# Moving half of chunk 1's index products into the first MLP group, and four weight subtractions to VectorE

## What is computed

```python
dots = jnp.einsum('bqhd,bsd->bqhs', iqb, ik) * IDX_DIM ** -0.5
score = jnp.einsum('bqh,bqhs->bqs', iwb, jax.nn.relu(dots))
score = jnp.where(causal[None], score, -jnp.inf)
_, idx = lax.top_k(score, k_sel)                      # k_sel = 256
...
mix = jnp.concatenate([pool_out, attn_out], axis=-1) @ w_o[l]
x = layer_norm(ALPHA * x + mix, ln1_g[l], ln1_b[l])
ff = jnp.square(jax.nn.relu(x @ w_up[l])) @ w_down[l]
x = layer_norm(ALPHA * x + ff, ln2_g[l], ln2_b[l])
```

## Time and profile before

| | us |
|---|---|
| median of 3 runs | 1300.05 (1298.27 to 1300.18) |
| profiled execution | 1294.91 |
| its span | 1292.9 |
| TensorE busy | 1217.0 (94%) |
| VectorE busy | 849.8 (66%) |
| ScalarE busy | 557.8 (43%) |
| GpSimd busy | 502.6 (39%) |
| mean granted TensorE clock | 0.982 |

### The profile page before, as it was taken

One profiled execution on the slowest core, in us unless ns is written; L12 is line 12 of the kernel. 1 busy time (PEld: TensorE's weight loads), 2 busy tenths in 40 slices (PEclk: granted clock), 3 DMA queues, 4 the chain that ended last, 5 costly groups with the idle time before them and its releaser, 6 DMA issues.

```text
span 1292.9 us, 17124 instructions
## 1 busy us (share of the span) xinstructions
PE 1217.0 (94%) x5639; PEld 975.7 (75%) x5639; DVE 849.8 (66%) x1322; ACT 557.8 (43%) x943; POOL 502.6 (39%) x366
## 2 busy tenths in 40 slices
PE   4999899799989999999999999989799999999997
PEld 2786686577668878778778778878688888888886
DVE  7677999766988888888989068953632232232337
ACT  3445652575525325334244266652243342442440
POOL 5534674333326666666666653204101101102002
PEclk9999899899989999999999999999899999999999
DMA  6732232030302222232332300224033323323331
GB/s 198 238 82 57 58 98 98 23 141 34 98 1 82 98 83 96 90 99 89 96 97 85 126 2 17 95 86 121 12 97 98 97 87 92 97 97 89 91 128 67
DMA packets 125724, 114.32 MB, mean 88 GB/s; under 512 B 5661, under 2 KB 99434, under 8 KB 125674
## 3 DMA queue, kind: packets, MB, share of 16 engines
q1 hardware_dynamic: 125674, 113.67, 28.2%
HBM read 105.25 MB, written 8.40 MB: 88 GB/s over the span
## 4 chain that ended last, share of the span: by engine, by line
PE 70%; DVE 16%; issue 7%; POOL 3%; ACT 2%; DVEq 1%; DMA 1%; POOLq 0%; SPq 0%; ACTq 0%
PE g_bank L1447 12%; PE g_bank L1448 12%; PE g_bank L1449 12%; PE wide L1447 10%; PE wide L1449 10%; PE wide L1448 10%; DVE score L866 3%; PE g_bank L1412 3%; DVE logit L927 1%; DVE win L548 1%; POOL rstd L703 1%; DVE probs_lo L943 1%; PE wide L1550 1%; DVE work L893 1%; POOL wo_lo L413 1%
## 5 line engine op out<-in xcount | busy, mean ns | idle before, releaser
L413 POOL TENSOR_TENSOR wlo<-wring,whi 128x1024 fp32r<-128x1024 f32 (+1 forms) x94 | 228.7, 2434 | 254.2 <-ACT whi L1331 128.6
L1447 PE MATMUL g_bank<-xhi,whi 128*128 128x512 f32 (+1 forms) x736 | 297.8, 405 | 5.5 <-DVE xlo L578 2.7
L1448 PE MATMUL g_bank<-xlo,whi 128*128 128x512 f32 (+1 forms) x736 | 293.7, 399 | 0.0
L1449 PE MATMUL g_bank<-xhi,wlo 128*128 128x512 f32 (+1 forms) x736 | 293.2, 398 | 0.0
L1331 ACT ACTIVATE whi<-wring 128x1024 fp32r<-128x1024 f32 x120 | 127.1, 1059 | 376.8 <-PE g_bank L1449 195.7
L413 DVE TENSOR_TENSOR wlo<-wring,whi 128x1024 fp32r<-128x1024 f32 (+1 forms) x66 | 88.3, 1339 | 224.6 <-ACT whi L1331 217.6
L1447 PE MATMUL wide<-whi,hhi 128*128 128x512 f32 x480 | 190.0, 396 | 1.0 <-POOL wlo L413 1.0
L1449 PE MATMUL wide<-whi,hlo 128*128 128x512 f32 x480 | 189.6, 395 | 0.0
L1448 PE MATMUL wide<-wlo,hhi 128*128 128x512 f32 x480 | 189.6, 395 | 0.0
L1447 PEld LDWEIGHTS g_bank<-xhi,whi 128*128 128x128 f32 (+1 forms) x736 | 138.9, 189 | 45.5 <-issue 5.4
L748 POOL TENSOR_TENSOR rows<-rows,y_stage 128x512 f32<-128x512 f32 x56 | 73.8, 1341 | 249.3 <-ACT y_stage L1321 248.0
(11 more groups left out here) (199 smaller groups left out, 1982.2 us busy)
## 6 DMA issues: line engine op xcount, KB each, us to landing
wring<-in_w_up SPq DMA_DIRECT2D x64, 512.0 KB, 4.2
wring<-in_w_down SPq DMA_DIRECT2D x64, 512.0 KB, 3.5
wring<-in_w_in SPq DMA_DIRECT2D x26, 512.0 KB, 3.8
wring<-in_w_o SPq DMA_DIRECT2D x16, 512.0 KB, 3.6
rows<-in_x SPq DMA_DIRECT2D x8, 512.0 KB, 4.7
normalized_rows<-rows SPq DMA_DIRECT2D x8, 512.0 KB, 4.3
rows<-normalized_rows SPq DMA_DIRECT2D x8, 512.0 KB, 6.2
out<-rows SPq DMA_DIRECT2D x7, 512.0 KB, 2.6
```

The costliest lines, as they stand in the source:

```text
L413: eng.tensor_tensor(parts_of(name, lo_tile(name)), parts_of(name, wring[n % 4]), parts_of(name, hi_tile(name)).bitcast(F32), ALU.subtract) ...
L1447: nc.tensor.matmul(out_ap, w_hi, m_hi, start=first, stop=False)
L1448: nc.tensor.matmul(out_ap, w_hi, m_lo, start=False, stop=False)
L1449: return nc.tensor.matmul(out_ap, w_lo, m_hi, start=False, stop=last)
```

## The change

1. Of the 32 index products of blocks 4 to 7, 16 stay in the output projection of chunk 0: one behind each step of half A, head by head (heads 0 to 3, each for blocks 4 to 7). The other 16 (heads 4 to 7) go into the first four up units of that chunk's MLP: three between accumulation pairs of the unit, one behind it. For this the first group is written out on TensorE, ScalarE and GpSimd (`past` and `dotted`), and its loops run one group less.
2. VectorE makes the last 16 additions after the whole residual stage and before the selections. An addition waits for that of the same block four before. GpSimd's diagonals move from before the MLP to its unit 4, behind all 48 additions; ScalarE waits for those at unit 4 too.
3. `relu_sb` moves to 40 to 48, where hidden parts 4 to 7 are written, and its neighbours to 32 to 40.
4. The parked weights of the output projection get places by chunk: in chunk 1 they lie at 32 to 64, and their high parts no longer wait for the low parts of the mix.
5. In chunk 1 the low parts of these four are made by VectorE, behind step (0, 2, 3), not by GpSimd.

```diff
-        relu_sb = part("relu_sb", 32, [P, 2, S])
-        near_up = part("near_up", 40, [P, HEADS, NEAR])
+        relu_sb = part("relu_sb", 40, [P, 2, S])
+        near_up = part("near_up", 32, [P, HEADS, NEAR])
...
-        park_at = (40, 44, 64, 68, 72, 76, 88.25, 92.25)
+        park_at = ((32, 36, 64, 68, 72, 76, 88.25, 92.25), (32, 36, 40, 44, 48, 52, 56, 60))
...
-                  or n[:2] == ("mlp", 1)]
+                  or n[:2] == ("mlp", 1) or n[:3] == ("wo", 1, 1)]
...
+        def dot_of(n):
+
+            return (n // HEADS + 2, n % HEADS) if n < 16 else ((n - 16) % CB + CB, (n - 16) // CB)
+
         def dots_after(c, nh, u, b):
 
-
-            counts = [1, 2] * 8 + [1] * 8 + [0] * 8
-            n = projection_steps().index((nh, u, b))
-            first = 16 + sum(counts[:n])
-            return [] if c else list(range(first, first + counts[n]))
+            return [16 + 4 * u + b] if c == 0 and nh == 0 else []
...
-                    pool.wait_ge(score_added, 8 * (i - 2) + 8)
+                    pool.wait_ge(score_added, 8 * (i - 2) + 8 if i < CB else 48)
...
-            diagonals((4, 5, 6, 7))
...
-            with pool.Fori(0, GROUPS - 1) as g:
+            def first_group(j):
+                if j == 4:
+                    diagonals((4, 5, 6, 7))
+                add_at(0, 0)(j)
+
+            mlp_lo(pool, 0, 0, False, first_group)
+            with pool.Fori(1, GROUPS - 1) as g:
                 mlp_lo(pool, 0, g, False, add_at(0, g))
...
-            lo(*units[U[("wo", 1, 0, 2)]:U[("mlp", 1, 0)]])
+            lo(("wo", 1, 0, 2), ("wo", 1, 0, 3))
...
-                    dve.wait_ge(score_added, n)
+                    dve.wait_ge(score_added, n if n < 16 else n - CB + 1)
...
+                    if c and (nh, u, b) == (0, 2, CB - 1):
+                        for piece in range(4):
+                            split_lo(dve, ("wo", 1, 1, piece), lo_dve)
...
             add_residual(0, LN1_0)
+            for d in range(32, 48):
+                add_score(d)
             for i in range(CB, NB):
                 select(i)
...
-                    act.wait_ge(mix_lo_ready, 8 * name[1] + 8)
+                    if name[1] == 0:
+                        act.wait_ge(mix_lo_ready, 8)
                     act.wait_ge(logits_full, 32 * name[1] + 32)
...
                     nh, u = divmod(j - GT, 4)
+                    if dotted and j < 4:
+                        for d in range(32 + 4 * j, 36 + 4 * j):
+                            relu_dots(d)
+                    if dotted and j == 4:
+
+                        act.wait_ge(score_added, 48)
...
-                act.wait_ge(score_added, 48)
-                with act.Fori(0, GROUPS - 1) as g:
-                    mlp(c, g, False)
+                if c == 0:
+                    mlp(0, 0, False, dotted=True)
+                with act.Fori(0, GROUPS - 2 + c) as g:
+                    mlp(c, g, False, 1 - c)
                 mlp(c, GROUPS - 1, True)
...
                 for k in range(KT):
+                    if dots and k and k % 2 == 0:
+                        dot(dots[k // 2 - 1])
...
-                        column_products(g_bank[(base + j) % 4][:, :], slot, ("x1T", c) if j == 0 else None)\
+                        dots = range(32 + 4 * j, 36 + 4 * j) if dotted and j < 4 else ()
+                        column_products(g_bank[(base + j) % 4][:, :], slot, ("x1T", c) if j == 0 else None, dots)\
                             .then_inc(g_full, 1)
+                        if dots:
+                            dot(dots[3])
                         continue
...
-                pe.wait_ge(relu_ready, 48)
                 pe.wait_ge(masked, 32 * c + 32)
-                with pe.Fori(0, GROUPS - c) as g:
-                    mlp(c, g, False)
+                if c == 0:
+                    mlp(0, 0, False, dotted=True)
+                with pe.Fori(0, GROUPS - 1) as g:
+                    mlp(c, g, False, 1 - c)
```

More of the change, by code:

```diff
@@ L181, in layer @@
         qlat_lo = part("qlat_lo", 48, [P, HEADS, CHUNK], F32R)
-        relu_sb = part("relu_sb", 32, [P, 2, S])
-        near_up = part("near_up", 40, [P, HEADS, NEAR])
[L184 to L187, removed]
+        relu_sb = part("relu_sb", 40, [P, 2, S])
+        near_up = part("near_up", 32, [P, HEADS, NEAR])
+        wuk_raw = part("wuk_raw", 32, [P, HEADS * HD])
+        hots = part("hots", 34, [NBUCKET, FWIN])
+        bias_row = part("bias_row", 35.5, [HEADS, FWIN])
+        vec_rows = part("vec_rows", 37, [37, P])
         hhi = part("hhi", 32, [P, GT, CHUNK], F32R)
@@ L203, in layer @@
         y_stage = part("y_stage", 72, [P, CB, 512])
-        park_at = (40, 44, 64, 68, 72, 76, 88.25, 92.25)
-        wo_hi = [part(f"wo_hi{u}", park_at[2 * u], [P, D], F32R) for u in range(4)]
-        wo_lo = [part(f"wo_lo{u}", park_at[2 * u + 1], [P, D], F32R) for u in range(4)]
+        park_at = ((32, 36, 64, 68, 72, 76, 88.25, 92.25), (32, 36, 40, 44, 48, 52, 56, 60))
+        wo_hi = [[part(f"wo_hi{c}{u}", park_at[c][2 * u], [P, D], F32R) for u in range(4)] for c in range(2)]
+        wo_lo = [[part(f"wo_lo{c}{u}", park_at[c][2 * u + 1], [P, D], F32R) for u in range(4)] for c in range(2)]
         end_hi = [part(f"end_hi{u}", 4 * u, [P, D], F32R) for u in range(4)]
@@ L852, in add_score @@
             def add_score(n):
-                i, h = n // HEADS + 2, n % HEADS
+                i, h = dot_of(n)
                 length = (i + 1) * P
@@ L1211, in relu_dots @@
             def relu_dots(n):
-                i = n // HEADS + 2
+                i = dot_of(n)[0]
                 act.wait_ge(dots_full, n + 1)
@@ L1307, in output_projection, with mlp @@
                 x1_hi(c, 1, range(4))
-            def mlp(c, g, last):
-                base, evacs, first = G[("mlp", c, 0)], EV[("mlp", c, 0)], U[("mlp", c, 0)]
+            def mlp(c, g, last, past=0, dotted=False):
+                base, evacs, first = G[("mlp", c, 0)], EV[("mlp", c, 0)] + GT * past, U[("mlp", c, 0)] + GUNITS * past
                 for j in range(GUNITS):
                     nh, u = divmod(j - GT, 4)
+                    if dotted and j < 4:
[3 more added lines that the diff above has]
+                        act.wait_ge(score_added, 48)
                     if j >= GT and u == 3 and not (c == 1 and last):
                         for b in range(CB):
-                            n = 8 * GROUPS * c + 4 * nh + b
+                            n = 8 * (GROUPS * c + past) + 4 * nh + b
                             act.wait_ge(wide_full, g * 8 + (n + 1))
@@ L1645, in down_products, with mlp @@
                 return last
-            def mlp(c, g, last_group):
-                base, evacs = G[("mlp", c, 0)], EV[("mlp", c, 0)]
+            def mlp(c, g, last_group, past=0, dotted=False):
+                base, evacs = G[("mlp", c, 0)], EV[("mlp", c, 0)] + GT * past
                 sem_lo, lo_base = LO[("mlp", c, 0)]
+                lo_base, seen = lo_base + GUNITS * past, GROUPS * c + past
                 split = R[("mlp", c, 0)]
@@ L1658, in mlp @@
                         pe.wait_ge(g_evac, g * GT + (evacs + j - 4))
-                        column_products(g_bank[(base + j) % 4][:, :], slot, ("x1T", c) if j == 0 else None)\
+                        dots = range(32 + 4 * j, 36 + 4 * j) if dotted and j < 4 else ()
+                        column_products(g_bank[(base + j) % 4][:, :], slot, ("x1T", c) if j == 0 else None, dots)\
                             .then_inc(g_full, 1)
+                        if dots:
+                            dot(dots[3])
                         continue
                     nh, u = divmod(j - GT, 4)
+                    if dotted and j == GT:
+                        pe.wait_ge(relu_ready, 48)
                     if nh == 0:
-                        pe.wait_ge(h_lo_ready[c], g * GT + (2 * u + 2 + 2))
+                        pe.wait_ge(h_lo_ready[c], g * GT + (GT * past + 2 * u + 2 + 2))
                     for b in range(CB):
                         if u == 0:
-                            pe.wait_ge(y_evac, g * 8 + (8 * GROUPS * c + 4 * nh + b + 1))
+                            pe.wait_ge(y_evac, g * 8 + (8 * seen + 4 * nh + b + 1))
                         last = down_products(c, g, nh, b, u, whi[slot], wlo[slot])
```

16 lines of the change are left out of this document (8 added, 8 removed).

## The result

The changed kernel takes **1286.74 us** (median of 4 runs, 1285.26 to 1287.88); the kernel before took 1299.16 us in the same session (4 runs). The ratio is 0.9908 [0.9893, 0.9924]. The profiled execution took 1285.83 us.

What follows compares the result with a forecast made beforehand. TensorE bounds the kernel, so time comes only from its gaps around the output projections. Terms -16.1 + 12.6 - 3.3 = -6.8 us give 1288.1 us profiled, 1293.3 us as median with the 5.1 us offset; range 1288.0 to 1298.0 us.

Steps and rivals of the forecast that it cites:

- I expect the same offset: Whole kernel: median 5.1 us above the profiled execution, as before, so 1288.1 us profiled becomes 1293.3 us.
- Part 1: Chunk 0's output projection: half of the index products leave it, so the MLP starts 16.1 us earlier.
- rival A: Chunk 0's projection: shared ports cost less than walked through, MLP starts 19.6 us earlier, 1289.7 us; chance 0.20.
- only behind it in its queue stands the relu: End of the projection's first half: ScalarE's MLP split delays the last relu, so VectorE's last addition ends at 46.5 us.
- Part 2: Chunk 0's MLP: 16 index products between the first four up units cost TensorE 12.6 us more.
- the unit of small margin: MLP unit 6 of chunk 0: its low part is ready at 45.7 us, wanted at 46.2; cost zero, 0.5 us to spare.
- Part 3: VectorE's selections start about 42 us after the MLP instead of 1.7; costs nothing, 7.4 us of waiting left.
- Rival C: Start of chunk 1's attention: VectorE's selections become the bound; slower from 14.2 us further delay, 1305.9 us with 20; chance 0.06.
- Part 4: Chunk 1's projection: VectorE makes the four parked low parts, loads issue 3.6 us earlier, saving 3.3 us.
- Rivals B: Chunk 0 gains nothing through worse backlog, unit 6 or port; chunk 1's gain remains, 1296.8 us; chance 0.18.
- D: Whole change: the edits do nothing because the tail's gap moves along whole, 1300 us; chance 0.01.

Runs made afterwards that it cites:

- each part alone: Changed kernel with GpSimd making chunk 1's parked low parts as before: 1290.4 us; kernel before with only those low parts moved to VectorE: 1293.23 us.
- twelve searches: Changed kernel plus twelve unused VectorE searches for maxima ahead of the selections: 1296.31 us, ratio 0.9987 to the kernel before.
- chunk 0 alone: Changed kernel with GpSimd making the low parts of chunk 1's four parked units as before: 1290.4 us, ratio 0.9938 to the kernel before.
- three edits in a row: Changed kernel plus, cumulatively, chunk 0's four parked low parts on VectorE, relu ahead of MLP load, inverse deviation between MLP low parts: 1286.07, 1287.01, 1288.37 us.

## Why the prediction was right and wrong

**Direction and mechanism: right.** TensorE's gaps around the projections were the reserve; chunk 0's projection gives back more than its MLP takes, and chunk 1 adds its part. The runs with each part alone show both.

**The step that failed is "I expect the same offset".** I took the profiled execution of before as 5.1 us quicker than its median, and gave the changed kernel the same. In the changed kernel the two are 0.9 us apart. Of the 6.6 us by which the forecast was too high, 4.2 are this step and 2.3 the terms (1288.1 forecast for the profiled execution, 1285.83 measured): parts 1, 2 and 4 gave 1.7, 1.1 and 0.3 more than said, and T0 came 1.1 later. The offset is no property of the kernel: 5.1 was one execution without the clock drop at T0, beside three runs; the same program's next profile lay 3.2 us above its median. The three runs were also on the slow side: in the three later sets, on three chips, the median of before was 1297.45 to 1298.0 us, 2.5 to 3.1 above that profile. With 0.9 for the offset my terms give 1289.0 us, inside the range, and still 2.3 too high: the rest is the size of the terms.

**Part 1, -16.1 forecast, -17.8 measured.** Half A ran without a stall, in exactly the 35.0 us of its rows; I had given it 0.9 of waits. GpSimd's last parked subtraction ended at 35.0, not 36.3. It was not lengthened (2.40 us): it had started first, at 329.02, and the addition that it met, at 329.63, was held instead (2.47 us for 640 columns). And the MLP load was split at 39.9 instead of 41.7. What stands behind moved with that: block 0 44.4 instead of 46.5, block 3 61.2 instead of 63.3. That is the ground of rival A (ports cost less), about half way to it. My sentence that "only behind it in its queue stands the relu" is what the trace shows, but as a cause it was wrong: VectorE itself was busy until 0.27 us before that relu came, and putting the relu first changed nothing. Three near-equal limits lie on one another there: VectorE's backlog, the MLP load, the port turns with its low parts.

**Part 2, +12.6 forecast, +11.5 measured.** The 16 products cost what their columns said: from the first MLP product to the first of the down units it is 57.55 us instead of 44.88, 12.7 more, and the unit of small margin did not stall TensorE. From there to the last MLP product it is 314.53 instead of 315.88, 1.35 less. What I left out: the one wait that the stage had before, of 1.0 us, fell, by the times of the rows, where GpSimd's four additions of `y` (448.14, 6.23 us) met VectorE's masking of block 4's scores (449.13). With the selections 40 us later the first such four take 5.07 us, and the row is gone. It is there in all three profiles of the old order (1.0, 1.1 and 1.0 us), and in none of the changed kernel's three. I had the 1 us in the earlier trace rows, and counted it as a cover rather than asking whether it would stay. TensorE's waits of before in that stage hold it:

```profile
PE wide L1447 <- POOL wlo L413: 1.0, 1, 1.0
```

**Part 3, nothing: right.** The first selection copy came 41.5 us after the MLP started (42 said), and 8.0 us were left (7.4 said). Rival C, the slower case, had its mechanism right, as twelve searches show, but not its price: I let it decide from 14.2 us of delay, the 7.4 to spare and the 6.8 gained, and 11.3 us of delay already cost 9.1.

**Part 4, -3.3: right** in the profiles (-3.6, and 3.1 alone). VectorE's parked low parts ended at 884.3, SP issued 0.3 us later, and block 0 came 29.4 us after the chunk's first projection product, where it came 33.3 before: 3.9 us, 3.5 said.

**Rivals B and D** fall: chunk 0 alone gains 0.62% [0.48, 0.75].

The range failed with the offset: it was built from bounds of the terms alone, and had nothing for the scatter of the one execution that all of them were set against. Its low end lay a little under rival A's time; the terms came out between my forecast and rival A, and only the offset put the result below both.

## To carry to other kernels

Set a sum of differences against the median of several runs, and ask of the profiled execution first whether its thin stretches ran at the full clock; four us that ran mostly at half clock cost 1.1 to 1.6 us here, as much as an edit may bring. Moving work out of a stage where three engines must answer each other, into one where a single engine is always busy and the others have room, can pay even though TensorE does the same work; here it brought 0.6%. When an edit behind such a move brings nothing, look for the next limit before giving up on it, but stop when successive limits share one resource: three edits in a row moved a hold by the ports from one operation to the next for 0.7 us in all.

## What was not expected of the hardware

The granted clock at the short thin stretches differs between executions of one program: at 296 to 300 us it was 1.00 in eight profiles and 0.57 to 0.62 in six, worth 1.1 to 1.6 us: with it half B began, in the changed order, 36.1 to 36.6 us after T0 instead of 35.0. TensorE's way there was a thin stretch of the same work each time. The six with the drop have T0 at 296.26 to 297.32 us, the eight without it at 295.33 to 296.43, so a later T0 goes with it; which of the two brings the other is not shown. At 745 to 750 it was 0.66 in two runs of the changed order and 0.50 behind the longest gap, 1.00 in the others. What decides it between equal programs stays open, and so does whether the change itself makes the drop at T0 rarer: the changed kernel's three profiles are free of it, but four of the eight experiments that share its code up to that point are not.
